# Two narrow weight tiles at the start of a float32 decoder kernel, and its last two output tiles and final norm in token halves

## The reference

```python
def rms_norm(x, w):
    y = xf * lax.rsqrt(jnp.mean(xf * xf, axis=-1, keepdims=True) + EPS)
    return (y * w.astype(jnp.float32)).astype(x.dtype)
...
    proj = h @ w_in                       # first layer, h = rms_norm(x, a_norm_pre)
    q, f, i, g = jnp.split(proj, [HGRN_FDIM, 2 * HGRN_FDIM, 2 * HGRN_FDIM + D_MODEL], axis=-1)
...
        h = rmsnorm(x, norm_ffn[i])
        x = x + jnp.square(jax.nn.relu(h @ w_up[i])) @ w_down[i]
    return rmsnorm(x, norm_final)
```

## Time and profile before

| | |
|---|---|
| median of 3 runs | 2532.42 us (2531.89 to 2533.18) |
| the profiled execution: its time, its span | 2532.29 us, 2530.5 us |
| TensorE busy | 2467.6 us, 98% of the span |
| VectorE, ScalarE, GpSimd busy | 1465.0 us (58%), 1168.2 us (46%), 159.5 us (6%) |
| DMA | 243.42 MB, mean 96 GB/s |
| first slice of 63 us | 155 GB/s |
| chain that ended last | TensorE 80%, VectorE 11%, ScalarE 6%, issue 3% |

### The profile page before, as it was taken

One profiled execution on the slowest core, in us unless ns is written; L12 is line 12 of the kernel. 1 busy time (PEld: TensorE's weight loads), 2 busy tenths in 40 slices (PEclk: granted clock), 3 DMA queues, 4 the chain that ended last, 5 costly groups with the idle time before them and its releaser, 6 DMA issues.

```text
span 2530.5 us, 35862 instructions
## 1 busy us (share of the span) xinstructions
PE 2467.6 (98%) x14408; PEld 2009.4 (79%) x14408; DVE 1465.0 (58%) x2366; ACT 1168.2 (46%) x2091; POOL 159.5 (6%) x156
## 2 busy tenths in 40 slices
PE   9999999999999999999989999999999999999998
PEld 6888778888777678888867878888877877888886
DVE  6665554433656564344378898877676556543343
ACT  5354353322456644233247676666455444432232
POOL 2110110000100010000000111111000010100001
PEclk9999999999999999999999999999999999999999
DMA  5222234534322223333324333333322233233322
GB/s 155 76 60 76 59 102 113 131 104 119 95 87 82 67 68 106 93 100 90 102 61 142 97 108 114 109 105 121 105 66 67 98 120 100 78 105 100 95 96 75
DMA packets 201782, 243.42 MB, mean 96 GB/s; under 512 B 8081, under 2 KB 133297, under 8 KB 201361
## 3 DMA queue, kind: packets, MB, share of 16 engines
q1 hardware_dynamic: 201616, 241.12, 32.0%
HBM read 231.00 MB, written 9.57 MB: 95 GB/s over the span
## 4 chain that ended last, share of the span: by engine, by line
PE 80%; DVE 11%; ACT 6%; issue 3%; DMA 0%; POOL 0%; DVEq 0%; SPq 0%; ACTq 0%; POOLq 0%
PE bank L1987 23%; PE bank L1989 22%; PE bank L1988 22%; DVE CV L2696 2%; DVE wlo L2471 1%; PE bank L1993 1%; PE bank L1995 1%; PE bank L1994 1%; PE bank L2006 1%; ACT whi L2256 1%; PE bank L2188 1%; DVE h L2505 1%; PE bank L2196 1%; PE bank L2209 1%; PE bank L2101 1%
## 5 line engine op out<-in xcount | busy, mean ns | idle before, releaser
L2471 DVE TENSOR_TENSOR wlo<-raw,whi 128x1024 fp32r<-128x1024 f32 x389 | 489.3, 1264 | 647.6 <-ACT whi L2256 645.1
L2256 ACT ACTIVATE whi<-raw 128x1024 fp32r<-128x1024 f32 x389 | 406.8, 1053 | 580.8 <-PE bank L1989 569.1
L1987 PE MATMUL bank<-XAh,whi 128*128 128x512 f32 x1552 | 616.6, 397 | 6.4 <-DVE XAl L2479 3.4
L1989 PE MATMUL bank<-XAh,wlo 128*128 128x512 f32 x1552 | 602.4, 388 | 0.0
L1988 PE MATMUL bank<-XAl,whi 128*128 128x512 f32 x1552 | 602.3, 388 | 0.0
L1987 PEld LDWEIGHTS bank<-XAh,whi 128*128 128x128 f32 x1552 | 292.3, 188 | 79.0 <-issue 11.8
L1989 PEld LDWEIGHTS bank<-XAh,wlo 128*128 128x128 f32 x1552 | 292.0, 188 | 61.4
L1988 PEld LDWEIGHTS bank<-XAl,whi 128*128 128x128 f32 x1552 | 292.3, 188 | 57.6 <-issue 1.0
L1987 PE MATMUL bank<-XBh,whi 128*128 128x512 f32 (+1 forms) x840 | 331.6, 395 | 1.8 <-DVE XBl L2477 1.7
L1989 PE MATMUL bank<-XBh,wlo 128*128 128x512 f32 (+1 forms) x840 | 324.0, 386 | 0.0
L1988 PE MATMUL bank<-XBl,whi 128*128 128x512 f32 (+1 forms) x840 | 323.8, 385 | 0.0
(11 more groups left out here) (330 smaller groups left out, 3258.7 us busy)
## 6 DMA issues: line engine op xcount, KB each, us to landing
raw<-in_w_in SPq DMA_DIRECT2D x77, 512.0 KB, 4.0
raw<-in_up SPq DMA_DIRECT2D x64, 512.0 KB, 3.7
raw<-in_down SPq DMA_DIRECT2D x64, 512.0 KB, 3.7
raw<-in_a_w_in SPq DMA_DIRECT2D x32, 512.0 KB, 4.1
E<-scr_rows SPq DMA_DIRECT2D x32, 512.0 KB, 5.5
raw<-in_w_up SPq DMA_DIRECT2D x32, 512.0 KB, 3.6
raw<-in_w_down SPq DMA_DIRECT2D x32, 512.0 KB, 3.6
raw<-in_w_kv SPq DMA_DIRECT2D x16, 512.0 KB, 3.6
```

The costliest lines, as they stand in the source:

```text
L1987: pe.matmul(out, wh[:, w, c], xh[:, x, r], start=st, stop=False)
L1989: m = pe.matmul(out, wl[:, w, c], xh[:, x, r], start=False, stop=en)
L2256: act.activation(s.hi, s.raw, ACT.Copy).then_inc(s.whi[0], 1)
L2471: dve.tensor_tensor(s.lo, s.raw, s.hi.bitcast(F32), ALU.subtract).then_inc(s.wlo[0], 1)
```

## The change

1. `gemm` gets a parameter `fine`: the first `fine` values of k have units of their own. The V product's first weight tile (k = 0 and 1, 512 KB) becomes two units of 256 KB, so that V's first half has units 0 (k = 0), 1 (k = 1) and 2 (k = 2, 3). FQ1 and FQ2 are now units 3 and 4. The product of k = 0 is planned behind the split of k = 0.
2. The first DMAs are ordered anew: weights k = 0, x 0, weights k = 1, x 1, weights k = 2 and 3, x 2 to 5, the weights of FQ1, x 6 and 7, and then the constants. `load_tab` (160 KB) is planned later.
3. The loop that places the splits is as it was, and its numbers now meet other units: at unit 2 (k = 2, 3) it places the splits of units 3 and 4, FQ1 and FQ2.
4. The last two output tiles are products over 256 tokens: tile 6 and tile 7 for tokens 0 to 255, then for tokens 256 to 511, in a new function `finish`. Square 6 has its own ones-matmul instead of the addition on VectorE. The factor of the first half and its scaling and stores are placed beside the products of the second half. The stores are two of 4 tiles x 256 tokens and four of 2 tiles x 256 tokens.

```diff
-    def gemm(X, nk, name, cols, jobs, evac, k0=0, x0=0, ntok=S, ring=ring_g, gate=None, pack=1, piece=None, halves=False):
+    def gemm(X, nk, name, cols, jobs, evac, k0=0, x0=0, ntok=S, ring=ring_g, gate=None, pack=1, piece=None, halves=False, fine=0):
...
-        for kk in range(0, nk, step):
-            n = min(step, nk - kk)
+        for kk in [*range(fine), *range(fine, nk, step)]:
+            n = 1 if kk < fine else min(step, nk - kk)
...
-        add("load_tab", land=sig("tab_in", 16))
-        K.tab_in = (p.sems["tab_in"], 16)
...
-            return gemm((XB, XA)[hf], 8, "a_w_in", [(2048 + hf * 512, 512)], [("tm", 0, 512)], v_evac(hf), ring=ring_h if hf else ring_g)
+            return gemm((XB, XA)[hf], 8, "a_w_in", [(2048 + hf * 512, 512)], [("tm", 0, 512)], v_evac(hf), ring=ring_h if hf else ring_g, fine=0 if hf else 2)
...
-            if k in (1, 3):
+            if k in (0, 1, 3):
                 next(g0)
...
         rcol_ready = s1.done
+        add("load_tab", land=sig("tab_in", 16))
+        K.tab_in = (p.sems["tab_in"], 16)
...
-                for k0, n in ((0, 4), (4, 4)) if qt < 3 else ((0, 4), (4, 2), (6, 1), (7, 1))[:3 if post is not None else 4]:
+                for k0, n in ((0, 4), (4, 4)) if qt < 3 else ((0, 4), (4, 2), (6, 1))[:3 if post is not None else 2]:
...
+            else:
+                finish(us[1], down, 24)
...
+    def finish(X, name, k0):
+        u = [(name, k0, 8, ((k * P, P),)) for k in (6, 7)]
+        n0 = len(p.units)
+        parts = [(tile_of(whi, (n0 + i) % NW, u[i]), tile_of(wlo, (n0 + i) % NW, u[i])) for i in range(2)]
+        p.units.extend(u)
+        bs = [[ring_all.take() for _ in range(2)] for _ in range(2)]
+        rb, r, qs = [ring_all.take() for _ in range(2)], rrs.take(), [sqs.take() for _ in range(2)]
+        at, sq, rt = [ht[6], ht[7]], {}, [None, None]
+        def product(i, x, lo=0, hi=8):
+            done = [sig("unit")] if hi == 8 else []
+            p.pieces += 1
+            add("unit", n=n0 + i, parts=parts[i:i + 1], per=8, at=lo, nk=hi - lo, kk=lo, total=8, ntok=256, c0=256 * x,
+                outs=[Step(job=("fm", 0), i=0, bank=bs[i][x], at=0)], done=done, xh=X.hi, xl=X.lo, x0=0, x_ready=list(X.ready), ends=bool(done), begins=lo == 0)
+            if not done:
+                return
+            if x:
+                p.unit_done.append(done[0])
+            c = HALVES[x]
+            ht[6 + i] = e = add("mix", mx=h[:, 6 + i, c], bank=bs[i][x], cols=c, unit=done[0], mx_free=[at[i]], plus=True, mix=sig("mix")).mix
+            bs[i][x].free(e)
+            sq[i, x] = add("sq", src=h[:, 6 + i, c], src_ready=e, q=qs[i], c0=x * 256, n=256, sq=sig("sq")).sq
+        def ones_of(q, sq, x, first=False, final=False):
+            return add("ones", q=q, sq=sq, bank=rb[x], c0=x * 256, n=256, first=first, final=final, ones=sig("ones")).ones
+        def factor(x, m):
+            rt[x] = add("rfin", bank=rb[x], ones=m, r=r, c0=x * 256, n=256, dim=D, rfin=sig("rfin")).rfin
+            rb[x].free(rt[x])
+        def scale(x, ks):
+            c = HALVES[x]
+            for k in ks:
+                f = add("final", h=h[:, k, c], gain=col(gain["norm_final_2"] + k), r=r.t[:, c], rfin=rt[x], h_ready=ht[k], scaled=sig("final"))
+            return f.scaled
+        def store(x, k, n, scaled):
+            add("store", out=out_d[:, k:k + n, HALVES[x]], h=h[:, k:k + n, HALVES[x]], scaled=scaled, land=sig("out", 16))
+        product(0, 0)
+        product(1, 0)
+        for x in range(2):
+            ones_of(last_tile.sum(), last_tile.added(), x, first=True)
+        product(0, 1, 0, 4)
+        ones_of(qs[0], sq[0, 0], 0)
+        factor(0, ones_of(qs[1], sq[1, 0], 0, final=True))
+        scale(0, (0, 1))
+        product(0, 1, 4, 8)
+        store(0, 0, 4, scale(0, (2, 3)))
+        product(1, 1, 0, 4)
+        ones_of(qs[0], sq[0, 1], 1)
+        store(0, 4, 4, scale(0, (4, 5, 6, 7)))
+        product(1, 1, 4, 8)
+        factor(1, ones_of(qs[1], sq[1, 1], 1, final=True))
+        for k in range(0, 8, 2):
+            store(1, k, 2, scale(1, (k, k + 1)))
...
-    order = [load_gain, p.order[0]] + loads[0] + load_x[0:2] + loads[1] + load_x[2:4] + loads[2] + load_x[4:6] + [load_cst] + load_x[6:8] + [splits[0]] + loads[NRAW]
+    order = [load_gain, p.order[0]] + loads[0] + load_x[0:1] + loads[1] + load_x[1:2] + loads[2] + load_x[2:6] + [splits[0]] + loads[NRAW] + load_x[6:8] + [load_cst]
```

More of the change, by code:

```diff
@@ L453, in tile @@
             return sq
[L455 to L460, removed]
+        tile.sum, tile.added = lambda: st["sum"], lambda: st["added"]
         def half(x, src, ready):
@@ L549, in make_plan @@
     HALVES = slice(0, 256), slice(256, S)
-    def mix_halves(mx, bk, m, mx_free, plus):
-        return [add("mix", mx=mx[:, c], bank=bk, cols=c, unit=m, mx_free=mx_free, plus=plus, mix=sig("mix")).mix for c in HALVES]
-    halves_of_h = {}
     def post_norm(mx, g):
@@ L957, in make_plan, with mlp @@
         end = [ht[7], p.unit_done[-1], XA.ready[7], XB.after[0]]
-    def mlp(up, down, post, begun, squares, ones, nxt, then=None, pre=None, then_ring=ring_all):
+    def mlp(up, down, post, begun, squares, ones, nxt, then=None, pre=None, then_ring=ring_all, finish=None):
         nonlocal end
@@ L998, in evac @@
                             yield from evac_p(k, b, m, [at[k]], True)
[L999 to L1005, removed]
                             return
@@ L1910, in make_plan @@
     both.close()
[L1911 to L1926, removed]
+    last_tile, _ = norm_sum(8)
@@ L1929, in make_plan @@
+    mlp("w_up_2", "w_down_2", None, begun, squares, ones, lambda k: last_tile(hsrc(k), ht[k]), finish=finish)
     loads, splits = [], []
```

## The result

| | before | changed kernel |
|---|---|---|
| median of 7 runs each | 2532.42 us (2531.36 to 2533.18) | 2539.16 us (2538.93 to 2541.21) |
| ratio | | 1.0028, 95% interval 1.0019 to 1.0037 |
| the profiled execution: its time, its span | 2532.29, 2530.5 us | 2538.93, 2537.1 us |

The changed kernel is 6.7 us slower; forecast were 2539.0 and 6.7. The total came out, but some of its terms did not, and their errors cancelled.

What follows compares the result with a forecast made beforehand. TensorE, busy 98% of the span, was taken to bound the kernel, leaving only its first and last 25 us to change. Start 4.0, clock 2.1 and end 0.6 gave 6.7 on 2532.3: 2539.0 us, 8 in 10 within 2533.5 to 2541.5.

Steps and rivals of the forecast that it cites:

- The cause: Start: FQ2's split ahead of k = 4 waits for its tile until 18.35; the start costs 3.5 to 4.6 us.
- FQ2's tile lands early: Start: rival with the tile landed by about 14.6, XBl of k = 4 ending near 17.9, 2532.3 us; chance 0.11.
- Wrong at V: Start: the halved unit 0 lets V begin 1.4 us earlier, at 7.1 instead of 8.49.
- the last rival: Start: the early V start brings nothing, or at most 1 us if the tile is early; no separate chance.
- Collision with GpSimd: Start: XBl of k = 4 beside a GpSimd addition takes 1.1 us more, ending between 21.4 and 22.5.
- The gap: Start: TensorE waits 1 to 2 us before k = 4 of FQ1 and 3.2 us before k = 5.
- The clock: After the start's gap: granted clock falls to half, costing 2.1 us, bounds 0 to 2.8; chance 0.48.
- The end: Last two tiles: products +0.6, ones-matmuls +2.2, square 6 +0.1, scalings -2.3; together +0.6 us.
- The rival with a bad end: End: six scalings delay tile 7's second half and half-row stores are slow; 2541.2 us with fallen clock; chance 0.07.

Runs made afterwards that it cites:

- early_fq2: Changed kernel with FQ2's load moved ahead of x 6 and 7 and the constants, its split left in place; 2534.62 us, ratio 1.0009.
- head_only: Changed kernel's start with the old end of the kernel before; 2540.19 us, ratio 1.0027.
- late_split_sqv: Changed kernel with FQ2's split back behind k = 7 and the first norm's squares added on VectorE instead of GpSimd; 2532.76 us, ratio 1.0000.
- best_head_old_end: The start of late_split_sqv with the old end of the kernel before; 2532.54 us, ratio 0.9999.
- filled_gap: Changed kernel with 18 extra matmuls into an unused bank ahead of k = 5 of FQ1; 2537.51 us, ratio 1.0020.
- tail_only: Kernel before with only the new end, its old start kept; 2533.49 us, ratio 1.0004.
- late_split: Changed kernel with only FQ2's split placed behind k = 7 again; 2532.95 us, ratio 1.0002.

## Why the prediction was right in its total

**The cause was named rightly, and is shown.** The prediction let FQ2's tile land at 18.35 and ScalarE wait for it; it landed at 18.54, and taking away the wait in two unlike ways took away 6.2 and 4.5 of the 6.7 us. The rival "FQ2's tile lands early" failed on the landing. So did its way there: the Trainium skill, DMA: Bandwidth & Descriptors, section Queues, rings and completion order, does not promise completion in order, but this tile, the last of the list, landed 8.3 us after its issue, with nothing won.

**Wrong at V.** V was to start at 7.1; it started at about 8.0, and its 0.2 us wait for XBl of k = 2 took back more. The step looked only at the operands and not at TensorE's own warm-up matmuls, which ended at 8.02 here and at 6.68 in the kernel before. That differs between executions: in early_fq2 and head_only V's second matmul came at 7.08 and 7.23, about where the step had it. So FQ1's k = 4 began 0.2 us earlier than before (21.98 against 22.18), not 1.4. That the early V start brings nothing, the last rival, is what happened. late_split_sqv and best_head_old_end, with late splits and no additions on GpSimd, show what it could bring: 0.6 and 0.9 us at the ones-matmuls.

**Collision with GpSimd: right in size, wrong in place.** XBl of k = 4 ended at 21.55, the low end of 21.4 to 22.5. The 1.1 us came one instruction later, on the 128x64 product, 1.31 instead of 0.21, and delayed k = 5 all the same. The Trainium skill, GPSIMD Engine Reference, section Key points, says that GpSimd contends with VectorE instructions that read two SBUF inputs. The trace agrees for the instruction that was held, which has two. XBl of k = 4 has two as well, began 0.04 us ahead of the addition and took 0.75, while the addition took 1.86; in early_fq2 it began 0.03 us ahead and took 1.87, while the addition took 1.29. The section does not say which of the two is held, and the runs show both, by starts that on GpSimd are rough.

**The gap: one, not two.** The sum had a wait of 1 to 2 us before k = 4 and 3.2 before k = 5. As V began later than thought, TensorE was still busy at 21.5, the first wait did not exist and the second was 4.0. In head_only, where V began early, both waits are there, 0.6 and 4.2. The end of XBl of k = 7 at 28.66 was just past the forecast's 28.6, and without the clock's fall the ones-matmuls come at 29.28 (filled_gap), which is 29.5 with the 0.25 of its profile taken out. Against 24.90 in the kernel before that is 4.6 us, and 4.7 at `Vg`: the upper end of 3.5 to 4.6, where the middle of 4.0 was taken.

**The clock: fell as forecast, cost half of it.** 2.1 was the forecast, 1.1 the measurement. The step took 5.6 us at half clock after the resumption, from the other fall in the trace, and it was 3.4; and it charged every slow matmul in full, though TensorE would have waited for XBl of k = 7 in part of that time. Two readings in it were off as well: 0.72 on average in the row at 1407 puts that fall at about 1407.4, not 1407.7, and a unit that ends at 30.3 is 1.2 late against its own 25.06 + 4.0, not 1.4. The bounds of 0 to 2.8 held. In head_only the same instructions paid more: the stretch to `Vg` was 1.3 us longer, 0.3 of it because XBl of k = 5 came later. And the changed kernel's profile is of its fastest run, 2538.93; two of its seven took 2541.2, and no profile shows their clock.

**The end: +0.1 instead of +0.6.** By the parts: products with ones-matmuls +2.9 (forecast +2.8), the chain to the first scaling 0 to +0.1, eight scalings 3.25 against 5.67, -2.4 (forecast -2.3), and from the last scaling to the span's end 2.8 us against 3.2. The last part had been held unchanged. The rival with a bad end fell: VectorE's six scalings did not delay tile 7's second half, since VectorE was idle for 0.29 us ahead of its addition, and the half-row stores of 256 KB landed in 2.2.

**Missing: the middle.** 0.7 us came where no instruction differs. The changed kernel's clock fell in two places, near 673 and 1304 us, where the profile before shows 1.00. The waits just ahead of both are in the two profiles alike: 1.05 and 2.17 us in the changed kernel, 1.04 and 2.18 in the kernel before, where they end at 667.00 and 1298.57. Twelve kernels with the same middle took 2459.9 to 2463.8 us for it. Whether the 0.7 follows from the shifted start or is chance from one execution to the next was not tested, with one profile per kernel; but 33 executions of the kernel before alone took 2530.82 to 2534.53 us, which is spread enough for it.

In short: 4.7 + 1.1 give the 5.8 at the start; 0.1 and 0.7 follow. The forecast 4.0 + 2.1 + 0.6 hit the sum by luck: a clock term that was 1.0 too large and an end that was 0.5 too large stood against a wait that was 0.7 too small and 0.7 in the middle that was left out. As a total, 2539.0 is better than its working deserved.

## What to carry to other kernels

A number of units as a look-ahead ("splits two units ahead") changes its meaning when units are made smaller: before cutting a tile, list what each in-order engine now meets first, and compare with when that data lands. An early split of a tile that lands late costs the wait on every instruction behind it, and the load has to move up with it, or neither. Ones-matmuls between products cost TensorE time, here 0.43 us each, that they do not cost behind the last product, where it would wait anyway.

## What the runs showed of the hardware that was not expected

- The same start, instruction for instruction, had a fall of the granted clock of 3.4 us in one execution (changed kernel) and of some 6.8 us in another (head_only), from about 26.0. TensorE had waited 4.0 us in the first, and 0.6 and 4.2 us with one k between in the second.
- The clock also fell after shorter waits: after one of 2.07 us at 2046.9 in tail_only and one of 2.17 at 1304.2 in the changed kernel. In the kernel before it stayed at 1.00 after the latter wait, 2.18 us there, so the wait alone does not decide it. Over the kernels, the same middle differed by 3.9 us.
- The eight rows of the warm-up matmuls, all of whose operands are there from 1.4 us on, took 5.23 us in the kernel before and 6.56 in the changed kernel, and 5.3 to 6.7 in the other ten. The last of them start 0.43 us apart in the first and 0.85 in the second, with 1.00 as the granted clock in both.
- An addition of 128x512 on GpSimd made one VectorE instruction that ran beside it 1.0 to 1.1 us longer, at either size seen: 0.74 to 1.77 for 128x512 (late_split), 0.21 to 1.31 for 128x64 (changed kernel). In the latter case XBl, which began 0.04 us ahead of the addition, was not lengthened, and the addition took 1.86 us.
- Eight scalings of 128x256 that stand together take 3.25 us, 0.41 each.
